# Two more places for expert weight blocks in the first round of a mixture-of-experts stage

## The reference

```python
h = rms_norm(x, norm_mix)          # three mixers on one input projection, merged by gates
x = x + merged @ w_out
x = x + memory_cross_attention(rms_norm(x, norm_xattn), rms_norm(mem, norm_mem), ...)
x = x + grouped_moe(rms_norm(x, norm_ffn), router_w, router_b, w_gate, w_up, w_down)
```

```python
for e in range(16):
    a = silu(h @ w_gate[e]) * (h @ w_up[e])        # 1024 -> 512, twice
    out = out + gates[..., e:e + 1] * (a @ w_down[e])   # 512 -> 1024
```

## Time and profile before

| | us |
|---|---|
| median of 3 runs | 566.31 |
| lowest, highest | 566.18, 567.34 |
| the profiled execution, its own time | 566.53 |
| span of that execution in the profile | 564.6 |
| PE busy | 551.7 (98% of the span) |
| DVE busy | 327.6 (58%) |
| ACT busy | 234.7 (42%) |
| POOL busy | 20.8 (4%) |

### The profile page before, as it was taken

The page is one execution under the profiler, slowest core; times in us unless marked ns, Lnnn a source line. Parts: engine busy times, 40 slices in busy tenths (PEclk is TensorE's granted clock), DMA queues, the critical chain, the costliest instruction groups (busy, mean ns, idle before and its releaser), DMA issues.

```text
span 564.6 us, 7184 instructions
## 1 busy us (share of the span) xinstructions
PE 551.7 (98%) x2745; PEld 364.5 (65%) x2745; DVE 327.6 (58%) x563; ACT 234.7 (42%) x315; POOL 20.8 (4%) x15
## 2 busy tenths in 40 slices
PE   8999999999998999999999999999999999999995
PEld 7789888888876778888888877533433443443333
DVE  5373686976578663789675645653444454443343
ACT  6663663674594554943636536211111111111112
POOL 0000000050020000000000102000000000000000
PEclk9999999999999999999999999999999999999999
DMA  8994674567543325676568699999999999999992
GB/s 312 406 314 158 216 269 150 167 250 252 170 167 112 111 76 186 240 247 221 171 203 297 229 369 426 380 400 425 427 425 427 425 427 425 427 425 427 427 419 98
DMA packets 46061, 165.19 MB, mean 293 GB/s; under 512 B 4292, under 2 KB 5448, under 8 KB 33480
## 3 DMA queue, kind: packets, MB, share of 16 engines
q1 hardware_dynamic: 43632, 158.85, 72.6%
q10 hardware_dynamic: 2392, 5.85, 2.9%
HBM read 163.63 MB, written 1.06 MB: 292 GB/s over the span
## 4 chain that ended last, share of the span: by engine, by line
PE 86%; DVE 4%; ACT 3%; DMA 2%; DVEq 1%; issue 1%; SPq 1%; POOL 0%; ACTq 0%; POOLq 0%
PE ps L2090 20%; PE ps L1638 15%; PE ps L1630 14%; PE ps L1631 14%; PE ps L2109 9%; PE ps L1611 3%; PE ps L2121 3%; PE ps L2004 2%; DMA w_raw<-in_w_in 2%; ACT w_hi L611 1%; PE ps L1807 1%; DVE w_lo L1022 1%; PE ps L1781 1%; PE ps L1995 1%; PE ps L1918 1%
## 5 line engine op out<-in xcount | busy, mean ns | idle before, releaser
L1022 DVE TENSOR_TENSOR w_lo<-w_raw,w_hi 128x2048 fp32r<-128x2048 f32 (+2 forms) x52 | 113.9, 2209 | 61.4 <-ACT w_hi L611 60.6
L1630 PE MATMUL ps<-w_hi,act_hi 128*128 128x512 f32 (+1 forms) x288 | 112.4, 392 | 0.4 <-ACT w_hi L611 0.4
L1631 PE MATMUL ps<-w_hi,act_lo 128*128 128x512 f32 (+1 forms) x288 | 110.1, 384 | 0.0
L611 ACT ACTIVATE w_hi<-w_raw 128x2048 fp32r<-128x2048 f32 (+2 forms) x52 | 95.1, 1854 | 32.8 <-PE ps L1638 7.7
L2090 PE MATMUL ps<-e_raw,xg 128*48 128x512 f32 x408 | 90.9, 594 | 0.0
L1638 PE MATMUL ps<-w_lo,act_hi 128*128 128x512 f32 (+1 forms) x288 | 70.3, 386 | 0.0
L2090 PEld LDWEIGHTS ps<-e_raw,xg 128*48 128x48 f32 x408 | 25.4, 123 | 57.4 <-issue 55.7
L1630 PEld LDWEIGHTS ps<-w_hi,act_hi 128*128 128x128 f32 x288 | 54.1, 188 | 11.8 <-issue 1.4
L1631 PEld LDWEIGHTS ps<-w_hi,act_lo 128*128 128x128 f32 x288 | 54.2, 188 | 10.0
L1638 PEld LDWEIGHTS ps<-w_lo,act_hi 128*128 128x128 f32 x288 | 52.6, 188 | 10.9 <-issue 0.7
L1515 DVE SCALAR_TENSOR_TENSOR a_tok<-ps,rs_slot,e_act 128x256 f32<-128x256 f32 x16 | 7.7, 484 | 73.9 <-ACT e_act L955 73.9
(11 more groups left out here) (290 smaller groups left out, 670.4 us busy)
## 6 DMA issues: line engine op xcount, KB each, us to landing
e_raw<-in_w_gate_up SPq DMA_DIRECT2D x51, 1024.0 KB, 16.3
w_raw<-in_w_in SPq DMA_DIRECT2D x30, 1024.0 KB, 5.3
e_raw<-in_w_expert_down SPq DMA_DIRECT2D x25, 1024.0 KB, 23.3
w_raw<-in_w_gate_up SPq DMA_DIRECT2D x13, 1024.0 KB, 21.3
w_raw<-in_w_expert_down SPq DMA_DIRECT2D x7, 1024.0 KB, 15.7
w_raw<-in_w_xkv SPq DMA_DIRECT2D x4, 1024.0 KB, 5.8
w_raw<-in_w_out SPq DMA_DIRECT2D x4, 1024.0 KB, 5.0
w_raw<-in_w_branch_b SPq DMA_DIRECT2D x4, 768.0 KB, 4.4
```

Source lines behind the costliest of these rows:

```text
L611: A(bview(w_hi, b, blocks[b].shape), bview(w_raw, b, blocks[b].shape), ACT.Copy).then_inc(hi_done, 1)
L1022: V.tensor_tensor(bview(w_lo, b, sh), bview(w_raw, b, sh), f32(bview(w_hi, b, sh)), ALU.subtract).then_inc(lo_done, 1)
L1630: MM(o, xh[:, t0 + k, i * P:(i + 1) * P], wh[:, k], start=first and k == 0, stop=False)
L1631: MM(o, xl[:, t0 + k, i * P:(i + 1) * P], wh[:, k], start=False, stop=False)
```

## The change

The first round gets 22 places in place of 20. Place 21 lies at `m_at` and holds block 2 alone; place 20 lies between `sel` and `h_lo`, where `selT` was. Places 18, 19 and 21 now hold one block each and don't return to the list. For that, several tensors move: `selT` to the bytes of place 18, once its block is used; `place_pairs` to those of place 21, once block 2 is used; `a_st` to the tail of the first gathered tile; the small tensors of the router to the place of `wT`. Two waits are added for it: ACT waits for the use of block 2 before it issues the two loads of `place_pairs`, and DVE for that of block 4, which lies in place 18, before it writes the first `selT`. On ACT, the wait for the number of rounds and its load into a register now stand ahead of these issues.

```diff
-FIRST_PLACES = (0, 1, 19, 18, 4, 5, 2, 3, 6, 7, 16, 8, 9, 10, 11, 12, 13, 14, 15, 17)
-FIRST_LOADS = (18, 4, 5, 2, 3, 6, 7, 19, 16, 8, 9, 10, 11, 12, 13, 14, 15, 17)
-ONCE = 19
+FIRST_PLACES = (0, 1, 21, 19, 18, 4, 5, 2, 3, 6, 7, 16, 8, 9, 10, 11, 12, 13, 14, 15, 20, 17)
+FIRST_LOADS = (18, 4, 21, 5, 2, 3, 6, 7, 19, 16, 8, 9, 10, 11, 12, 13, 14, 15, 20, 17)
+ONCE = (18, 19, 21)
...
-        a_st_at = place["at"]
-        a_st = [sb(f"a_st_{k}", [P, FF // P, LANES]) for k in range(2)]
...
+        a_st = [at(f"a_st_{k}", xg_at + 6144 + 1024 * k, [P, FF // P, LANES]) for k in range(2)]
...
+        sel_at = place["at"]
         sel = sb("sel", [P, NT, EPG, P], f32r)
-        selT = [sb(f"selT_{k}", [P, EPG, S], f32r) for k in range(2)]
+        place_20_at = region(8192)
         h_lo = sb("h_lo", [P, NT, D], f32r)
...
-        place["at"] = m_at
+        selT = [at(f"selT_{k}", spare_2_at + 4096 * k, [P, EPG, S], f32r) for k in range(2)]
+        place_pairs = [at(f"place_pairs_{k}", m_at + 4096 * k, [P, 2, EPG, S], bf16) for k in range(2)]
+        place["at"] = wT_at
...
-        places_at = region(4 * EPG * S), wT_at
-        place_pairs = [at(f"place_pairs_{k}", places_at[k], [P, 2, EPG, S], bf16) for k in range(2)]
...
-                  at("e_raw_18", spare_2_at, [P, BLK]), at("e_raw_19", xg_at + 8192, [P, BLK])]
+                  at("e_raw_18", spare_2_at, [P, BLK]), at("e_raw_19", xg_at + 8192, [P, BLK]),
+                  at("e_raw_20", place_20_at, [P, BLK]), at("e_raw_21", m_at, [P, BLK])]
...
-            free += [k for k in place_of[-1:] if k != ONCE]
+            free += [k for k in place_of[-1:] if k not in ONCE]
...
+                elif k == 20:
+                    sp.wait_ge(mm_done, NB1)
+                elif k in (5, 21):
+                    sp.wait_ge(mm_done, first_block[C_XQ + 1])
...
-                elif k == 5:
-                    sp.wait_ge(mm_done, first_block[C_XQ + 1])
...
             even_gathered(0)
+            act.wait_ge(s["rounds_ready"], 1)
+            rounds = act.value_load(n_rounds_i[0:1, 0:1], min_val=1, max_val=ROUNDS)
             act.wait_ge(s["rows_spread"], 16)
+            act.wait_ge(mm_done, NB1 + FIRST_PLACES.index(21) + 1)
             for k in range(2):
                 places_in(k)
-            act.wait_ge(s["rounds_ready"], 1)
-            rounds = act.value_load(n_rounds_i[0:1, 0:1], min_val=1, max_val=ROUNDS)
             with act.Fori(0, rounds) as r:
...
                         dve.wait_ge(s["rows_spread"], 16 * 3)
+                        dve.wait_ge(mm_done, NB1 + FIRST_PLACES.index(18) + 1)
                         turned_selection(0)
```

More of the change, by code:

```diff
@@ L256, in build_program @@
         xg = [at(f"xg_{k}", xg_at + 8192 * k, [P, KD, EPG, SLOTS]) for k in range(2)]
+        a_st = [at(f"a_st_{k}", xg_at + 6144 + 1024 * k, [P, FF // P, LANES]) for k in range(2)]
+        assert 4 * KD * EPG * SLOTS <= 6144
         x2T = at("x2T", xg_at, [P, KD, S])
@@ L259, in build_program @@
         h_hi = sb("h_hi", [P, NT, D], f32r)
+        sel_at = place["at"]
         sel = sb("sel", [P, NT, EPG, P], f32r)
-        selT = [sb(f"selT_{k}", [P, EPG, S], f32r) for k in range(2)]
+        place_20_at = region(8192)
         h_lo = sb("h_lo", [P, NT, D], f32r)
-        junk_2 = [at(f"junk_2_{k}", place["at"] + 2048 * k if k < 3 else a_st_at, [P, COLS]) for k in range(4)]
+        junk_2 = [at(f"junk_2_{k}", place["at"] + 2048 * k if k < 3 else sel_at, [P, COLS]) for k in range(4)]
         e_act = sb("e_act", [P, FF // 2])
@@ L269, in build_program @@
         assert place["at"] <= spare_2_at and spare_2_at % LINE == 0 and spare_2_at + 8192 == m_at, (place["at"], spare_2_at)
-        place["at"] = m_at
+        selT = [at(f"selT_{k}", spare_2_at + 4096 * k, [P, EPG, S], f32r) for k in range(2)]
+        place_pairs = [at(f"place_pairs_{k}", m_at + 4096 * k, [P, 2, EPG, S], bf16) for k in range(2)]
+        assert 8192 <= POST and not place_20_at % LINE
+        place["at"] = wT_at
         gates_split = sb("gates_split", [P, NT, 2, NE], f32r)
@@ L279, in build_program @@
         count_w, chosen_r = sb("count_w", [P, 2, P], f32r), sb("chosen_r", [P, NT, NE], f32r)
-        assert place["at"] <= m_at + POST, (place["at"], m_at)
         e_raw = [None] * RING + [at("e_raw_4", q_at, [P, BLK]), at("e_raw_5", m_at + POST, [P, BLK]), e_raw_6, e_raw_7]
@@ L324, in build_program @@
         s = {n: sem(n) for n in names}
-        e_in_slot += [s["x_pair_landed"], s["tile_0_landed"]]
+        e_in_slot += [s["x_pair_landed"], s["tile_0_landed"], s["tile_1_landed"], s["tile_2_landed"]]
         win = d_in["w_in"][0].rearrange("(p t) n -> p t n", t=KD)
@@ L479, in e_slot @@
             if k >= RING:
-                earlier = [0] * 4 + [16, 16] + [0] * 2 + list(LOADED.values()) + [16, 16]
+                earlier = [0] * 4 + [16, 16] + [0] * 2 + list(LOADED.values()) + [16] * 4
                 return e_raw[k], e_in_slot[k], earlier[k] + 16 * turns
```

## The result

| | before | after |
|---|---|---|
| median, 19 runs each, us | 566.52 | 567.45 |
| lowest to highest | 565.86 to 567.34 | 567.24 to 568.28 |
| the profiled execution, its own time | 566.53 | 567.46 |
| its span | 564.6 | 565.6 |

The ratio is 1.0018, with a 95% interval of 1.0011 to 1.0025: some 1.0 us slower (0.6 to 1.4), clear of no change and just inside the 0.2% that was called "within". The medians differ by 0.93 us. One execution among all that follow, of the last experiment, ran at a mean granted clock of 0.753 and took 700.75 us; it is in no ratio.

What follows compares the result with a forecast made beforehand. PE was taken to bound the expert stage, transfers having 1.7 us to spare. Terms 0 + 0 + 1.03 us on the median 566.31 gave 567.34, say 567.3 us; range 566.0 to 568.5.

Steps and rivals of the forecast that it cites:

- within: Outcome class for the whole kernel: time changed by no more than 0.2% (1.13 us); chance 0.53.
- What bounds the kernel: Expert stage: PE bounds it, no wait names a transfer, and some 1.7 us were to spare at block 93.
- Places 21 and 20: First-round block loads on SP: no new wait, extra block fits free DMA time before 325 us; worth 0.
- The new addresses: Turned selections, rows and small tiles moved: same instructions and shapes, DVE's wait for block 4 covered by 11 us; 0.
- ACT's wait: Start of expert stage: waiting for block 2 before the place_pairs loads makes Silu, and the end, 1.03 us late.
- second issue: ACT's second place_pairs load: holds ACT 0.58 us, between 0.46 (second of the mem_x pair) and 0.69 (before).
- end of the issues to the table load: ACT's loop entry, from register moves to the start of the table load: 0.5 us.
- table load, to Silu: ACT's table load before expert 0's Silu: 1.28 us, and 0.02 to the ACTIVATE.
- PE's gap: Predicted sign: about 1.2 us before expert 1's first matmul, with the waits naming a_tok.
- (b): Rival on ACT: issues hold it for hardly any time, Silu 0.1 us late, time 566.4; 13%.
- (c): Rival at the end: timed executions wait for transfers, so longer lead makes it faster, 563.9 at best, 565 likelier; 11%.
- (d): Rival: slower by more, ACT's issues held by a full queue or place_pairs landing after 380; 568.2 to 570; 18%.

Runs made afterwards that it cites:

- the last experiment: The kernel after with SP issuing the loads of place_pairs and ACT loading the Silu table early; ratio 1.0001 (0.9993 to 1.0010) to the kernel before.

## Why the prediction was right

*What bounds the kernel.* Right. The transfers had about 1.7 us to spare: taking one block of lead away cost 0.6 us (0.1 to 1.1; the medians differ by 0.8, and 2.46 less 1.7 is 0.8), taking three cost 6.1 (7.4 less 1.7 is 5.7). Adding one bought nothing measurable.

*Places 21 and 20.* Right in all its steps: the extra block went into the free time before 325 us, blocks 22 and 23 were issued from 358.48, and then SP stood until 370.54. The transfers did give part of the lead back: slice 27, 367.6 to 381.8 us, has 321 GB/s. The spare time did grow: block 93 was issued at 520.17 in place of 521.9 and landed 26.0 us later, at 546.2, and PE came to it at about 550.5, half-way through these matmuls:

```profile
548.70 3.60 PE L2115 MATMUL ps<-e_raw,a_st 128*64 128x512 f32 x16
```

That is 4.3 us to spare in place of 1.7; 1.0 of the difference is PE's own delay, the other 1.6 the longer lead.

*The new addresses.* 0, as predicted; shown with the added issues moved to SP, where all of the rest of the change is in place.

*ACT's wait.* Right in mechanism, and each term can be set beside its measure:

| term | predicted | seen |
|---|---|---|
| first issue to the next | 0.37 | 0.37 |
| second issue | 0.58 (0.46 to 0.69) | 0.46 |
| end of the issues to the table load | 0.50 | 0.49 |
| table load, to Silu | 1.30 | 1.29 |
| sum from the issue to Silu | 2.75 | 2.60 |

The mis-sized term is the second issue. It took what the second of the `mem_x` pair had taken; the 0.69 before fell together with an issue of SP (358.53), and no run here has that pair again, so that the one caused the other is only argued. With 19 and 17 places the traces have the two issues 1.6 to 1.8 us earlier, with no issue of SP beside them, and there the second took 0.45, which fits. With 0.46 the sum gives 0.91 us, against the medians' 0.93. PE's gap was called "about 1.2 us"; it is 1.0 on the matmuls and 1.1 on the weight loads. That the forecast of 567.3 lies only 0.15 from the measured 567.45 is in part luck: the stall was put 0.10 too high, on a median of three runs that was 0.21 below that of nineteen. The stall passed to the end one to one: Silu came 0.9 us late, expert 1 began at 366.86 in place of 365.97 and the span grew by 1.0. For other stalls the same holds nearly, as long as the clock stays: PE waits in the traces of 0.7, 1.0, 1.0, 1.4 and 1.7 us gave medians 0.6, 0.7, 0.9, 1.4 and 1.8 above those of before.

*The table load.* It costs its 1.28 us and nothing that can be seen beside them. After, the ACTIVATE stands 0.01 us behind the end of the load (364.52 + 1.28, and 365.81), against 0.02 in the earlier trace rows, and taking the load out from behind four issues took 1.27 us off (3.57 to 2.30). Between two ACTIVATEs that follow at once it is the same: with the early table and four issues the load starts at 356.75, 0.02 us behind the last gathered tile's ACTIVATE, and the Silu behind it at 358.04, 0.01 us behind the load's end.

*Rivals.* (b), issues that hold ACT for hardly any time, is refuted by the trace after, 0.82 us for two issues, and by the runs with three and four: each added one, of 256 KB, moves Silu by 0.48 to 0.49 us more (2.60, 3.08, 3.57), and the second of the two of 512 KB took 0.46 us and 0.03 to what follows it. (c), timed executions that wait for transfers at the end, is refuted by the times: one place fewer costs 0.6 to 0.8 us of the 2.46 of a block, so the timed executions too had some 1.7 us to spare with 20 places, and with 22 and no stall nothing is gained. (d): neither issue was held, with 0.34 and 0.46 us; the loads landed 5.5 and 7.1 us after their issue, and the first `selT` was written at 380.12, moved by PE's delay alone.

*What had not been seen.* The prediction let each microsecond of stall count once. In these runs that holds up to 1.4 us of PE's standing still; at 1.9 the fall of the clock took another 1.7 in the trace, and by mean clock and time in five of six executions.

## What to carry to other kernels

In these runs the wait put on ACT's queue cost what stands behind it up to Silu: 0.82 us for the two issues, 0.49 for the loop entry, 1.29 for the table load, and 0.76 for the register read where that was left behind the issues, each small and each formerly hidden. Add such times up before choosing the queue. Here SP had some 10 idle microseconds (from 360.52 to 370.54) for the same two issues, and ScalarE's idle time from 356.6 to 361.4 us had room for the table load. And before making room for more prefetch, look in the waits for one that names a transfer: without one, more places bought nothing here, though the spare time grew.

## What the hardware showed that was not expected

PE's clock behind its wait for `a_tok` at the start of expert 1. The wait and the lowest granted clock from 350 to 380 us are those of the trace; the mean clocks and times are those of every execution:

| run | PE's wait, us | lowest clock | executions |
|---|---|---|---|
| three issues | 1.4 | 1.00 | ten at 0.997 to 0.999, 567.35 to 568.47 us |
| the read left behind the issues | 1.7 | 1.00 | five at 0.998, 567.71 to 568.55 us; one at 0.995, 569.47 us |
| four issues | 1.9 | 0.50 | five at 0.995, 569.59 to 570.64 us; one at 0.998, 568.19 us |

In the trace with four issues the clock was at 0.50 for 3.4 us, and expert 1's 32 matmuls took 1.7 us more for it. Over 567.8 us that lowers the mean clock by 0.003, the step from 0.998 to 0.995. By that estimate the clock fell in five of the six executions, and in one of the six with the read left behind; the waits of the executions without a trace are taken to be those of the traced one. That the length of the wait decides is the author's reading of this table: no run varies the wait alone. The number of issues doesn't decide it: with four and the early table the wait was 0.7 us and the clock 1.00. Nor do DMA engines that have little to do: with four issues they moved 381 GB/s from 367.5 to 368 us, when the clock fell, and with three 97 GB/s from 368 to 372 us, at a clock of 1.00. In time, the 0.9 us more wait of four issues against two came with 2.5 us (3.5 against 1.0).

An issue of `place_pairs` on ACT took 0.34 us as the first and 0.45 to 0.47 right behind another, for 256 KB and 512 KB alike, in the traces of the kernel after and of eight experiments; the one exception is the 0.69 of the kernel before.
